# Block attention put between the blocks of two gate projections

## The chip, the cores and the metric

One core of one Trainium2 chip. The metric is the device time of one execution in microseconds (us): the median of three runs.

## What is computed

Two transformer-like blocks run one behind the other on 256 tokens of width 2048, all in float32. The first is latent attention and an mLSTM layer. The change lies in the second block:

```
mod  = silu(c) @ w_ada + b_ada                    # six rows of 2048, "ada"
h    = rms_norm(x, norm1) * (1 + sc1) + sh1
qa, ka, va, qb, kb, vb, ga, gb = split(h @ w_in)
ya   = softmax(qa ka' * scale) va                 # 8 heads on 2 key heads, all 256 keys
yb   = softmax(qb kb' * scale + bias) vb          # 8 heads, neighbourhood of 16 columns
merged = sigmoid(ga) * (ya @ w_oa) + sigmoid(gb) * (yb @ w_ob)
x    = x + g1 * (merged @ w_out)
```

A feed-forward layer of width 5632 and a last norm follow. Each head has 128 columns. A unit of the attention is one head and one of the two blocks of 128 queries, so there are 32 units.

## The kernel before

The weights of all projections come through one ring of four slots. A block is 128 rows by 1024 columns of a weight, 512 KB. SP (SyncE) loads it into `raw` when the slot was rounded the last time (`lo_ready`). ACT rounds it to `hi` (`hi_block`, line 545; it waits for the landing and until PE is done with the block four before). DVE writes what rounding left, `raw - hi`, to `lo` (`lo_block`, line 919). PE multiplies in three passes, hi x XH, lo x XH and hi x XL, where XH and XL are the two parts of the activations: 12 matmuls of 512 columns for a block (`token_major`, line 1644), which then counts `block_done`. Blocks are numbered through the kernel; `B_MERGE` is the first of the gates.

PSUM has eight banks of 512 columns. They are used as two halves, group 0 and group 1, of four banks. A projection accumulates in one half over 16 blocks, while the other half is evicted. `TURN_PLAN` (line 78) gives each projection its half (`@0` or `@1` sets it, else they alternate) and who evicts it. `start` (line 1634) makes PE wait until the last user of its half was evicted.

Beside the projections runs the ada product: 384 pieces of 128x512, 256 KB each, which POOL loads into a second ring of four slots (`ada_raw`) and DVE adds up, one instruction for a piece (`ada_block`, line 924). `ADA_BESIDE` (line 129) says how many pieces stand beside which projection; `rest_blocks` (line 954) spreads them over the blocks 4 to 15 of it, each behind the block's rounding. Pieces are taken in one fixed order, so a changed number moves all that follow.

All engines run lists written out by hand, with semaphores between them. Around the change the order is: the projections qa, kva, qb, kb, vb; the row g1; the transposes qaT and kaT; the attention (lines 1722 for PE, 629 for ACT, 1039 for DVE), which runs alone, with three of the four ring slots rounded, and uses all eight banks; then the four gate projections ga0, ga1, gb0 and gb1, with 16 blocks each; oa0, ob0, oa1 and ob1 with 8 each; the transposes of `merged`; and wo0 and wo1 with 16 each.

The attention is a pipeline over units. PE computes the scores (L1732), DVE adds the bias for units of b (L1505) and takes the maximum (L1048), ACT takes the exponential (L646), PE turns it (L1742), ACT copies it (L639), PE multiplies it with the values (L1753), DVE divides by the sum (L1053, L1063), PE turns the pair of a head back (L1762), and ACT and DVE write its two parts (L651, L1073).

The mLSTM stage has a similar pattern already: in mz0 and mz1 PE computes a head's scores (L1843, L1849, L1850) and values (L1864) behind every fourth block.

Of the kernel before, what the change touches and what calls it, by code (L numbers as in the profile page):

```python
# [13 lines left out]
P = 128  # L14
# [34 lines left out]
for _name, _n in (("ident", 128), ("inv_freq", 32), ("causal", 256), ("window", 64), ("toeplitz", 191),  # L49
# [36 lines left out]
    "biasa:act biasb:act ada1:dve hTa@1:split4 hTb:split4 qa:act kva:act qb:act kb:act vb:act g1:act qaT:act kaT:act "  # L86
    "ga0@0:act ga1:act gb0:act gb1:act oa0:dve ob0:dve oa1:dve ob1:dve mTa:split4 wo0:dve mTb:split4 wo1@0:dve "

# [35 lines left out]
for _name in GROUP:  # L124
    if _name not in LAST_BLOCK and _name not in BANKS_BEFORE:
# [4 lines left out]
              "mo_1": 20, "mz0": 6, "mz1": 6, "lo0": 16,  # L130
              "qa": 16, "kb": 8, "vb": 16, "ga0": 22, "ga1": 22, "gb0": 22, "gb1": 22, "oa0": 6, "ob0": 6, "oa1": 6,
              "ob1": 6, "wo0": 20, "wo1": 20}
ADA_FIRST = {}
for _name, _n in ADA_BESIDE.items():
    ADA_FIRST[_name] = sum(ADA_BESIDE[_m] for _m in ADA_FIRST)
N_UNITS = sum(ADA_BESIDE.values()) // KD


def two_block_kernel(nc, positions, x, xT, pack, const, gate_b, qk_norm, rpbT, mla_w_in, mla_w_qb, mla_w_kvb,
# [4 lines left out]
    with ExitStack() as ctx:  # L144
# [61 lines left out]
        vb_tok = at("vb_tok", 168, [P, TOK, N_A * HD])  # L206
        sig_a = at("sig_a", 168, [P, TOK, D])
        sig_b = at("sig_b", 184, [P, TOK, D])
        kva_tok = at("kva_tok", 176, [P, TOK, 4, HD])
# [3 lines left out]
        probT2 = at("probT2", 197, [P, 2, SEQ])  # L213
        y_tok2 = at("y_tok2", 199, [P, 4, P])
        merged = sig_a
# [88 lines left out]

        A1, A3 = att_sems("mla"), att_sems("blk")

        def bank(S, n):

            return ((n + 4) % 8 if S is A1 else n) * HALF
        M2 = {n: sem(f"ml_{n}") for n in ("prep", "prepc", "st", "bc", "arg", "exp", "w", "pv", "h", "sq", "y",  # L310
# [225 lines left out]
        def _(act):  # L536
# [92 lines left out]
            def attention(S, units, pr, prT, nm, rs, keys, H):  # L629

                for i in range(units + 6):
                    if 2 <= i < units + 2:
                        u = i - 2
                        nk = keys(u)
                        b = bank(S, 3 + u % 2)
                        act.wait_ge(S["turned"], u + 1)
                        if u >= 2:
                            act.wait_ge(S["summed"], u - 1)
                        nc.scalar.copy(prT[:, u % 2, 0:nk], ps[:, b:b + nk]).then_inc(S["copied"], 1)  # L639
                    if i < units:  # L640
                        u = i
                        nk = keys(u)
                        act.wait_ge(S["maxed"], u + 1)
                        if u >= 3:
                            act.wait_ge(S["turned"], u - 2)
                        nc.scalar.activation(pr[:, u % 3, 0:nk], ps[:, bank(S, u % 3):bank(S, u % 3) + nk], ACT.Exp,  # L646
                                             bias=nm[:, u:u + 1], accum_out=rs[:, u:u + 1]).then_inc(S["exped"], 1)
                    if i >= 6 and i % 2 == 0:
                        h = (i - 6) // 2
                        act.wait_ge(S["backed"], h + 1)  # L650
                        nc.scalar.copy(H(h), ps[:, bank(S, 7):bank(S, 7) + SEQ]).then_inc(S["hi"], 1)  # L651

# [156 lines left out]
            for tok in range(TOK):  # L809
# [27 lines left out]
            rest(B_MERGE, 16)  # L837
            for n, (name, sig) in enumerate((("ga0", sig_a), ("ga1", sig_a), ("gb0", sig_b), ("gb1", sig_b))):
                first4(B_MERGE + 16 * (n + 1))
                c0 = n % 2 * COLS  # L840
                each_tok(name, lambda t: sig[:, t, c0:c0 + COLS], ACT.Sigmoid)
                rest(B_MERGE + 16 * (n + 1), 16 if n < 3 else 8)
            for n in range(3):
# [60 lines left out]
        def _(dve):  # L904
# [48 lines left out]

            def rest_blocks(n0, b0, b1, nb, name=None, hooks=(), before=lambda b: None, beside=None):

# [83 lines left out]
            def attention(S, units, nm, rs, ri, yt, keys, prepare, gate, H, L):  # L1039
                inverse = {}  # L1040
                for i in range(units + 6):
                    if i < units:
                        u = i
                        nk = keys(u)
                        b = bank(S, u % 3)
                        dve.wait_ge(S["scored"], u + 1)
# [8 lines left out]
                    if 4 <= i < units + 4:  # L1055
                        u = i - 4
                        b = bank(S, 5 + u % 2)
                        after(inverse[u])
# [11 lines left out]
                    if i >= 7 and i % 2 == 1:  # L1070
                        h = (i - 7) // 2
                        dve.wait_ge(S["hi"], h + 1)
                        nc.vector.tensor_tensor(L(h), ps[:, bank(S, 7):bank(S, 7) + SEQ], H(h).bitcast(F32),  # L1073
                                                ALU.subtract) \
# [432 lines left out]

            attention(A3, 32, nmax2, rsum2, rinv2, y_tok2, lambda u: SEQ, add_bias, None,
                      lambda h: yaH[:, h, :] if h < N_A else ybH[:, h - N_A, :],
                      lambda h: yaL[:, h, :] if h < N_A else ybL[:, h - N_A, :])  # L1510
            lo_block(B_MERGE + 3, 3)
            rest(B_MERGE, 16, "ga0")
            for n, name in enumerate(("ga1", "gb0", "gb1")):
                first4(B_MERGE + 16 * (n + 1))
                rest(B_MERGE + 16 * (n + 1), 16, name)
            first4(B_MERGE + 64)
            rest(B_MERGE + 64, 8, "oa0")
            def merge_columns(name, q, first_tok):

                for tok in range(TOK):  # L1520
                    if tok == 0:
                        after(first_tok)
                    else:
                        dve.wait_ge(freed_sem["dve"], FREED[name][1])
                    m = merged[:, tok, q * COLS:(q + 1) * COLS]
                    nc.vector.tensor_tensor(m, m, sig_b[:, tok, q * COLS:(q + 1) * COLS], ALU.add) \
                      .then_inc(ev("merged"), 1)

            for n, name in enumerate(("oa0", "ob0", "oa1", "ob1")):
# [6 lines left out]
                for tok in range(TOK):  # L1536
                    v = sig[:, tok, q * COLS:(q + 1) * COLS]
                    ins = nc.vector.tensor_tensor(v, v, T(name, tok), ALU.mult)
# [92 lines left out]
        def _(pe):  # L1631
# [90 lines left out]
            def attention(S, units, pr, prT, yt, keys, operands, values):  # L1722
                for i in range(units + 6):
                    if i < units:
                        u = i
                        nk = keys(u)
                        b = bank(S, u % 3)
                        if u >= 3:
# [6 lines left out]
                    if 2 <= i < units + 2:  # L1735
                        u = i - 2
                        b = bank(S, 3 + u % 2)
                        pe.wait_ge(S["exped"], u + 1)
# [6 lines left out]
                    if 3 <= i < units + 3:  # L1745
                        u = i - 3
                        b = bank(S, 5 + u % 2)
                        pe.wait_ge(S["copied"], u + 1)
# [7 lines left out]
                    if i >= 6 and i % 2 == 0:  # L1756
# [4 lines left out]
                        for tok in range(TOK):  # L1761
                            ins = nc.tensor.transpose(ps[:, bank(S, 7) + tok * P:bank(S, 7) + (tok + 1) * P],  # L1762
                                                      yt[:, (2 * h + tok) % 4, :], ident[:, :])
# [159 lines left out]

            def blk_operands(u):
                h, blk = (u % 16) // 2, u % 2
                t = slice(blk * P, (blk + 1) * P)
                if u < 16:
                    return [(qaT[:, h, t], kaT[:, h // (N_A // N_KV), :])]
                return [(qbT[:, h, t], kbT[:, h, :])]

            def blk_values(u, t):
                h = (u % 16) // 2
                return kva_tok[:, t, N_KV + h // (N_A // N_KV), :] if u < 16 else vb_tok[:, t, h * HD:(h + 1) * HD]

            attention(A3, 32, prob2, probT2, y_tok2, lambda u: SEQ, blk_operands, blk_values)
            pe.wait_ge(A3["lo"], 16)
            for n, name in enumerate(("ga0", "ga1", "gb0", "gb1")):
                token_major(name, B_MERGE + 16 * n, 16, XH, XL)
# [3 lines left out]
            transposes("mTa", operand_tiles(merged, 0))  # L1942
# [3 lines left out]
            transposes("mTb", operand_tiles(merged, 8))  # L1946
            token_major("wo0", B_WO, 16, XH, XL, m_tiles, blocks=(5, 16))
# [104 lines left out]
```

## Time and profile before

| | |
|---|---|
| runs | 2322.74, 2323.46, 2320.55 us; median 2322.74 |
| profiled execution | 2328.05 us, its span 2326.0 us |
| mean granted TensorE clock | 0.978 |
| PE busy | 2242.2 us, 96% of the span |
| DVE busy | 1495.8 us, 64% |
| ACT busy | 1010.2 us, 43% |
| moved by the queues | 499.25 MB, mean 215 GB/s |

The span runs from the first to the last instruction of the program; the run's time has a few us around it. Busy shares are means over stages with different limits; the stages around the change are in the rows below. PE's busy time is modelled and overlaps from one matmul to the next, so the start times of the matmuls say more than the durations. In a row of busy time by stretch stand its start and end, its length, the busy time of PE, of PE's weight loads, DVE, ACT and POOL with the number of instructions, then the granted clock as a share of full speed, the busy share of the queues and their GB/s. In a row of a group stand its busy time and the mean ns of one instruction, then the idle time of the engine before them. In a timeline, x2 is two instructions put together, and one float32 matmul of the attention is two instructions.

### The profile page before, as it was taken

To read this page: it belongs to the slowest core of one execution; us is meant where nothing else is said; L and a number is where in the kernel's file an instruction comes from. 1 tells how busy PE (TensorE), PEld (TensorE's weight loads), DVE (VectorE), ACT (ScalarE), POOL (GpSimd) and SP (SyncE) were. 2 spreads that over 40 slices of the span, in tenths; PEclk is the share of its full clock that TensorE was granted. 3 is DMA by queue.
4 is the path that set the end of the run, shared out by engine and by line. 5 is a ranking of instruction groups with operands and counts; after the bars stand their busy time and mean duration, and the time that the engine had idled before them with its cause. 6 is when DMAs were issued, how large, how long until landed. Compare 5 with 4: busy or idle time off the path is not lost.

```text
span 2326.0 us, 33356 instructions
## 1 busy us (share of the span) xinstructions
PE 2242.2 (96%) x11044; PEld 1886.3 (81%) x11044; DVE 1495.8 (64%) x1990; ACT 1010.2 (43%) x1248; POOL 243.3 (10%) x425
## 2 busy tenths in 40 slices
PE   8999997999999979999999999989999999999997
PEld 6888776997877768899777878878888888888885
DVE  5666577897776866678677778875454444444544
ACT  5444534444444434443544433444344444443432
POOL 1110011212220030101112221110000000000000
PEclk9999999999999997999999999999999999999998
DMA  8786067787986583767449888764656656666563
GB/s 304 249 239 179 28 226 253 243 267 265 315 272 180 157 246 118 257 182 235 162 140 313 305 305 276 260 228 145 190 189 191 190 184 196 190 193 206 188 198 120
DMA packets 196667, 499.25 MB, mean 215 GB/s; under 512 B 29785, under 2 KB 56537, under 8 KB 195649
## 3 DMA queue, kind: packets, MB, share of 16 engines
q1 hardware_dynamic: 163648, 388.03, 51.6%
q0 software_dynamic: 32896, 109.55, 14.4%
q8 instruction: 82, 1.34, 0.2%
q14 instruction: 41, 0.33, 0.0%
HBM read 495.34 MB, written 2.10 MB: 214 GB/s over the span
## 4 chain that ended last, share of the span: by engine, by line
PE 74%; DMA 10%; DVE 8%; issue 4%; ACT 3%; POOL 1%; POOLq 0%; DVEq 0%; SPq 0%; ACTq 0%
PE ps L1663 59%; PE ps L1672 7%; DMA ada_raw<-in_w_ada_dram 7%; DVE lo L921 3%; PE ps L1732 2%; DVE acc_s L933 2%; DMA raw<-in_ml_w_in_dram 1%; PE ps L1753 1%; PE ps L1823 1%; ACT hi L549 1%; DVE acc_g L933 1%; PE ps L1742 1%; DMA raw<-in_w_in_dram 1%; DVE conv_tmp L1225 1%; DMA rel<-in_rpbT_dram 1%
## 5 line engine op out<-in xcount | busy, mean ns | idle before, releaser
L921 DVE TENSOR_TENSOR lo<-raw,hi 128x1024 fp32r<-128x1024 f32 x732 | 890.5, 1223 | 576.6 <-ACT hi L549 574.5
L549 ACT CAST hi<-raw 128x1024 fp32r<-128x1024 f32 x732 | 768.0, 1054 | 1089.3 <-PE ps L1663 770.2
L1663 PE MATMUL ps<-hi,XH 128*128 128x512 f32 x2080 | 652.3, 394 | 38.9 <-DVE lo L921 31.3
L1663 PE MATMUL ps<-lo,XH 128*128 128x512 f32 x2080 | 646.3, 391 | 0.0
L1663 PE MATMUL ps<-hi,XL 128*128 128x512 f32 x2080 | 645.4, 390 | 0.0
L1663 PEld LDWEIGHTS ps<-hi,XH 128*128 128x128 f32 x2080 | 388.5, 189 | 125.9 <-DVE lo L921 27.2
L1663 PEld LDWEIGHTS ps<-hi,XL 128*128 128x128 f32 x2080 | 392.1, 189 | 82.8
L1663 PEld LDWEIGHTS ps<-lo,XH 128*128 128x128 f32 x2080 | 392.1, 189 | 82.6
L463 POOL DMA_DIRECT2D ada_raw<-in_w_ada_dram x384 | 206.9, 539 | 1190.6 <-DVE acc_s L933 811.1
L933 DVE SCALAR_TENSOR_TENSOR acc_s<-ada_raw,c_act,acc_s 128x512 f32<-128x512 f32 x256 | 191.5, 748 | 47.2 <-DMA ada_raw<-in_w_ada_dram 45.0
L1672 PE MATMUL ps<-XH,hi 128*128 (+1 forms) x512 | 145.0, 283 | 1.1 <-DVE XL L1037 1.1
L1672 PE MATMUL ps<-XH,lo 128*128 (+1 forms) x512 | 144.9, 283 | 0.0
L1672 PE MATMUL ps<-XL,hi 128*128 (+1 forms) x512 | 144.9, 283 | 0.0
L933 DVE SCALAR_TENSOR_TENSOR acc_g<-ada_raw,c_act,acc_g 128x512 f32<-128x512 f32 x128 | 95.8, 749 | 37.4 <-DMA ada_raw<-in_w_ada_dram 36.6
L1663 PE MATMUL ps<-hi,FH 128*128 128x512 f32 x352 | 108.5, 389 | 0.0
L1663 PE MATMUL ps<-lo,FH 128*128 128x512 f32 x352 | 108.4, 389 | 0.0
L1663 PE MATMUL ps<-hi,FL 128*128 128x512 f32 x352 | 108.3, 389 | 0.0
L1672 PEld LDWEIGHTS ps<-XH,hi 128*128 128x128 f32 x512 | 98.3, 192 | 1.4 <-DVE XL L1037 1.4
L1672 PEld LDWEIGHTS ps<-XL,hi 128*128 128x128 f32 x512 | 98.3, 192 | 0.0
L1672 PEld LDWEIGHTS ps<-XH,lo 128*128 128x128 f32 x512 | 98.3, 192 | 0.0
L1663 PEld LDWEIGHTS ps<-lo,FH 128*128 128x128 f32 x352 | 66.1, 188 | 13.8
L1663 PEld LDWEIGHTS ps<-hi,FL 128*128 128x128 f32 x352 | 66.1, 188 | 13.7
(311 smaller groups left out, 1676.8 us busy)
## 6 DMA issues: line engine op xcount, KB each, us to landing
ada_raw<-in_w_ada_dram POOLq DMA_DIRECT2D x384, 256.0 KB, 5.1
raw<-in_w_in_dram SPq DMA_DIRECT2D x136, 512.0 KB, 4.6
raw<-in_ml_w_in_dram SPq DMA_DIRECT2D x128, 512.0 KB, 5.0
raw<-in_w_gate_dram SPq DMA_DIRECT2D x176, 256.0 KB, 2.8
raw<-in_w_up_dram SPq DMA_DIRECT2D x176, 256.0 KB, 3.0
raw<-in_w_down_dram SPq DMA_DIRECT2D x88, 512.0 KB, 3.7
raw<-in_mla_w_in_dram SPq DMA_DIRECT2D x48, 512.0 KB, 5.3
raw<-in_mla_w_out_dram SPq DMA_DIRECT2D x32, 512.0 KB, 4.7
```

What stands on the lines that cost most here:

```text
L463: pool.dma_start(ada_raw[:, j, :], w_ada[0][bass.ds((RING * g + j) * P, P), bass.ds(u * HALF, HALF)]) \
L549: nc.scalar.copy(hi[:, j, :], raw[:, j, :]).then_inc(hi_ready, 1)
L921: nc.vector.tensor_tensor(lo[:, j, :], raw[:, j, :], hi[:, j, :].bitcast(F32), ALU.subtract) \
L933: nc.vector.scalar_tensor_tensor(out=acc, in0=ada_raw[:, m % RING, :], scalar=c_act[:, k:k + 1], in1=acc, op0=ALU.mult, op1=ALU.add).then_ ...
L1225: ins = nc.vector.scalar_tensor_tensor(out=conv_tmp[:, k, s:], in0=ps[:, g + k * SEQ:g + (k + 1) * SEQ - s], scalar=col("conv_w", (TAPS - ...
L1663: ins = mm(ps[:, o:o + HALF], x, w[:, j, c0:c0 + HALF], start=first, stop=(k == nb * per_block - 1 and x is xl), skip_group_check=True)
L1672: ins = mm(ps[:, o:o + SEQ], w[:, j, m * P:(m + 1) * P], x(k), start=first and lead and m % 2 == 0, stop=last and w is lo, skip_group_chec ...
L1732: ins = mm(ps[:, b:b + nk], q, kk, start=(n == 0), stop=(n == len(ops) - 1), skip_group_check=True)
L1742: ins = nc.tensor.transpose(ps[:, b + t * P:b + (t + 1) * P], pr[:, u % 3, t * P:(t + 1) * P], ident[:, :])
L1753: ins = mm(ps[:, b:b + P], prT[:, u % 2, t * P:(t + 1) * P], values(u, t), start=(t == 0), stop=(t == n - 1), skip_group_check=True)
L1823: ins = mm(ps[:, o:o + 1], acc_s[:, vec, k * P:(k + 1) * P], ones[:, 0:1], start=True, stop=True, skip_group_check=True)
```

## The change

Attention and gates are merged into one stage. The attention is cut into 36 steps, which stand behind the first 31 gate blocks: one behind each, and two behind the blocks 3, 6, 9, 12 and 15. The units of b come first, then those of a.

In a step i, PE computes the scores of unit i, the values of head (i-4)/2 if i is even, and turns unit i-2. ACT rounds block b+4, then takes the exponential of unit i and, in odd steps, copies both turned units of a head in one instruction; in even steps it writes the high part of a head's result. DVE adds the bias and takes the maximum of unit i ahead of the rounding of block b+4, and behind this rounding and its ada pieces it divides unit i by its sum and, in odd steps, writes the low part of a result.

The division is now on the probabilities, 256 columns in SBUF, ahead of their transposes. The value matmuls have the values as weights and 256 queries as columns, so that the result comes out turned; the transposes back are gone. The attention needs four banks (4 to 7): two for scores, one for the turned probabilities, one for the result. The gates ga0, ga1 and gb0 all accumulate in group 0. The sigmoids of ga0 and ga1 are evicted ahead of the rounding of the blocks 19 and 35.

Ada pieces: ga0 has 12 instead of 22; qa has 18 instead of 16, kva 4 instead of none, and wo0 and wo1 have 22 each instead of 20. `sig_a`, `sig_b` and `merged` are laid out by column half first. The rest of the diff is the function `bank`, which has lost an argument.

```diff
-    "ga0@0:act ga1:act gb0:act gb1:act oa0:dve ..."
+    "ga0@0:act ga1@0:act gb0@0:act gb1:act oa0:dve ..."
-              "qa": 16, "kb": 8, "vb": 16, "ga0": 22, "ga1": 22, "gb0": 22, "gb1": 22, ... "wo0": 20, "wo1": 20}
+              "qa": 18, "kva": 4, "kb": 8, "vb": 16, "ga0": 12, "ga1": 22, "gb0": 22, "gb1": 22, ... "wo0": 22, "wo1": 22}
+STEPS_AFTER = {}
+_step = 0
+for _block in range(31):
+    _n = 2 if _block in (3, 6, 9, 12, 15) else 1
+    STEPS_AFTER[_block] = tuple(range(_step, _step + _n))
+    _step += _n
...
+        def score_slot(u):
+            return (4 + u % 2) * HALF
+        turn_slot, value_slot = 6 * HALF, 7 * HALF
...
@@ ACT
-            attention(A3, 32, prob2, probT2, nmax2, rsum2, lambda u: SEQ,
-                      lambda h: yaH[:, h, :] if h < N_A else ybH[:, h - N_A, :])
+            def blk_step(i):
+                if i < 32:
+                    act.wait_ge(A3["maxed"], i + 1)
+                    if i >= 3:
+                        act.wait_ge(A3["turned"], i - 2)
+                    o = score_slot(i)
+                    nc.scalar.activation(prob2[:, i % 3, :], ps[:, o:o + SEQ], ACT.Exp, bias=nmax2[:, i:i + 1],
+                                         accum_out=rsum2[:, i:i + 1]).then_inc(A3["exped"], 1)
+                if i >= 3 and i % 2 and i < 34:
+                    h = (i - 3) // 2
+                    act.wait_ge(A3["turned"], 2 * h + 2)
+                    if h:
+                        act.wait_ge(A3["summed"], h)
+                    nc.scalar.copy(probT2[:, :, :].rearrange(flat), ps[:, turn_slot:turn_slot + HALF]) \
+                      .then_inc(A3["copied"], 1)
+                if i >= 4 and i % 2 == 0:
+                    h = (i - 4) // 2
+                    H, _, hh = blk_head(h)
+                    act.wait_ge(A3["summed"], h + 1)
+                    nc.scalar.copy(H[:, hh, :], ps[:, value_slot:value_slot + SEQ]).then_inc(A3["hi"], 1)
...
+            for b in range(4, 48):
+                if b == 19:
+                    act.wait_ge(A3["summed"], N_A)
+                    gate("ga0", sig_a, 0)
+                if b == 35:
+                    act.wait_ge(A3["summed"], 2 * N_A)
+                    gate("ga1", sig_a, 1)
+                hi_block(B_MERGE + b, b % RING, landed(B_MERGE + b, b % RING))
+                for i in STEPS_AFTER.get(b - 4, ()):
+                    blk_step(i)
@@ DVE, rest_blocks
                     done = b - start - RING
                     for m in range(count * done // (nb - RING), count * (done + 1) // (nb - RING)):
                         ada_block((ADA_FIRST[name] + m) // KD, (ADA_FIRST[name] + m) % KD)
+                    behind(b)
@@ DVE
+            def blk_maximum(i):
+                if i < 32:
+                    o = score_slot(i)
+                    dve.wait_ge(A3["scored"], i + 1)
+                    add_bias(i, o)
+                    nc.vector.tensor_reduce(nmax2[:, i:i + 1], ps[:, o:o + SEQ], AX_X, ALU.max, negate=True) \
+                      .then_inc(A3["maxed"], 1)
+            def blk_divide(i):
+                if i < 32:
+                    dve.wait_ge(A3["exped"], i + 1)
+                    link(nc.vector.reciprocal(rinv2[:, i:i + 1], rsum2[:, i:i + 1]))
+                    nc.vector.tensor_scalar(prob2[:, i % 3, :], prob2[:, i % 3, :], rinv2[:, i:i + 1], None,
+                                            ALU.mult).then_inc(A3["normed"], 1)
+                if i >= 5 and i % 2:
+                    h = (i - 5) // 2
+                    H, L, hh = blk_head(h)
+                    dve.wait_ge(A3["hi"], h + 1)
+                    nc.vector.tensor_tensor(L[:, hh, :], ps[:, value_slot:value_slot + SEQ],
+                                            H[:, hh, :].bitcast(F32), ALU.subtract).then_inc(A3["lo"], 1)
...
@@ PE
+            def blk_step(i):
+                if i < 32:
+                    ...
+                    if i >= 2:
+                        pe.wait_ge(A3["exped"], i - 1)
+                    o = score_slot(i)
+                    mm(ps[:, o:o + SEQ], q, k, start=True, stop=True, skip_group_check=True).then_inc(A3["scored"], 1)
+                if i >= 4 and i % 2 == 0:
+                    h = (i - 4) // 2
+                    pe.wait_ge(A3["copied"], h + 1)
+                    if h >= 1:
+                        pe.wait_ge(A3["lo"], h)
+                    ...
+                        ins = mm(ps[:, o:o + SEQ], v, probT2[:, t, :], start=(t == 0), stop=(t == TOK - 1),
+                                 skip_group_check=True)
+                    ins.then_inc(A3["summed"], 1)
+                if 2 <= i < 34:
+                    u = i - 2
+                    pe.wait_ge(A3["normed"], u + 1)
+                    if u >= 2 and u % 2 == 0:
+                        pe.wait_ge(A3["copied"], u // 2)
+                    for t in range(TOK):
+                        o = turn_slot + t * SEQ + u % 2 * P
+                        ins = nc.tensor.transpose(ps[:, o:o + P], prob2[:, u % 3, t * P:(t + 1) * P], ident[:, :])
+                    ins.then_inc(A3["turned"], 1)
...
+            for n, name in enumerate(("ga0", "ga1", "gb0")):
+                token_major(name, B_MERGE + 16 * n, 16, XH, XL, then=blk_after(16 * n))
             pe.wait_ge(A3["lo"], 16)
```

## Rows read from the trace of the kernel before

**Rows 1.** Busy time by stretch: attention, two gates, two gates, wo.
```profile
1142.76:1187.32 44.56, 41.61 (x281) 34.92 (x280) 36.89 (x125) 31.26 (x109) 0.00 (x0) 0.99 0.01 2
1187.32:1279.35 92.03, 89.92 (x384) 72.92 (x385) 66.17 (x75) 36.39 (x35) 26.04 (x46) 0.98 0.83 286
1279.35:1371.25 91.90, 88.23 (x384) 71.72 (x385) 68.09 (x77) 37.17 (x36) 23.67 (x44) 1.00 0.89 306
...
1461.69:1558.00 96.31, 92.46 (x406) 74.55 (x407) 76.17 (x86) 37.57 (x40) 19.37 (x36) 1.00 0.77 260
```

**Rows 2.** Timeline of PE: start, duration; two units of attention, a gate block.
```profile
1144.31 0.60 PE L1732 MATMUL ps<-kaT,qaT 128*128 128x256 f32 x2
1144.74 0.38 PE L1742 MATMUL ps<-ident,prob 128*128 128x128 f32 x2
1144.96 0.61 PE L1753 MATMUL ps<-kva_tok,probT 128*128 128x128 f32 x4
...
1193.17 0.62 PE L1663 MATMUL ps<-hi,XH 128*128 128x512 f32 x2
...
1195.90 0.61 PE L1663 MATMUL ps<-hi,XH 128*128 128x512 f32 x2
```

**Rows 3.** Waits of PE in the gates: us in total, times, longest.
```profile
PE ps L1663 <- DVE lo L921: 5.6, 6, 1.6
```

**Rows 4.** Timeline of PE in mz0: one head between four blocks.
```profile
696.84 0.69 PE L1843 MATMUL ps<-ge,select 8*128 8x256 f32 x2
697.46 0.70 PE L1849 MATMUL ps<-qkT 128*128 128x256 f32 x2
698.00 0.38 PE L1850 MATMUL ps<-qkT 128*128 128x128 f32 x2
...
706.43 1.46 PE L1864 MATMUL ps<-mv,decay 128*128 128x257 f32 x6
...
710.54 0.69 PE L1843 MATMUL ps<-ge,select 8*128 8x256 f32 x2
```

**Rows 5.** Groups by line in the attention: count, busy us, mean ns.
```profile
L646 ACT ACTIVATE prob<-ps,nmax 128x256 f32<-128x256 f32 x30 | 14.3, 478 | 7.1 <-DVE nmax L1048 7.1
L1048 DVE TENSOR_REDUCE nmax<-ps 128x1 f32<-128x256 f32 x30 | 12.7, 425 | 6.0 <-PE ps L1732 5.3
...
L1505 DVE TENSOR_TENSOR ps<-ps,na_bias 128x256 f32<-128x256 f32 x16 | 9.5, 591 | 0.0
...
L646 ACT ACTIVATION_READ_ACCUMULATOR prob<-ps,nmax 128x1 f32 x30 | 5.9, 198 | 0.0
L1053 DVE RECIPROCAL rinv<-rsum 128x1 f32<-128x1 f32 x31 | 4.8, 153 | 0.0
...
L1073 DVE TENSOR_TENSOR ybL<-ps,ybH 128x256 fp32r<-128x256 f32 x8 | 3.4, 419 | 1.4 <-ACT ybH L651 1.4
```

**Rows 6.** Groups by line in the four gates: rounding and ada pieces.
```profile
L921 DVE TENSOR_TENSOR lo<-raw,hi 128x1024 fp32r<-128x1024 f32 x62 | 75.1, 1220 | 14.4 <-ACT hi L549 14.3
L549 ACT CAST hi<-raw 128x1024 fp32r<-128x1024 f32 x64 | 67.5, 1055 | 110.3 <-DMA raw<-in_w_in_dram 58.2 <-PE ps L1663 45.6 <-DMA raw<-in_w_oa_dram 6.5
L933 DVE SCALAR_TENSOR_TENSOR acc_s<-ada_raw,c_act,acc_s 128x512 f32<-128x512 f32 x88 | 65.9, 749 | 35.3 <-DMA ada_raw<-in_w_ada_dram 34.4
```

**Rows 7.** Timeline of ACT at the eviction of ga0.
```profile
1235.19 1.28 ACT L586 ACT_TABLE_LOAD   x1
1236.49 1.94 ACT L586 ACTIVATE sig_a<-ps 128x1024 f32<-128x1024 f32 x2
```

**Rows 8.** Groups by line elsewhere: a scaling in SBUF, a copy from PSUM.
```profile
L1408 DVE TENSOR_SCALAR h_norm<-X,ry 128x2048 f32<-128x2048 f32 x2 | 2.6, 1286 | 0.1
...
L806 ACT COPY na_bias<-ps 128x480 f32<-128x480 f32 x6 | 3.0, 569 | 8.0 <-PE ps L1906 8.0
```

**Rows 9.** Busy time by stretch, behind the tail and behind a wait.
```profile
1187.90:1191.80 3.90, 3.90 (x12) 3.03 (x11) 1.12 (x1) 0.00 (x0) 0.00 (x0) 0.56 0.39 105
...
1361.80:1365.80 4.00, 3.99 (x18) 3.28 (x19) 3.81 (x5) 1.13 (x2) 1.16 (x3) 1.00 0.83 273
```

More of the change, by code:

```diff
@@ L86 @@
     "biasa:act biasb:act ada1:dve hTa@1:split4 hTb:split4 qa:act kva:act qb:act kb:act vb:act g1:act qaT:act kaT:act "
-    "ga0@0:act ga1:act gb0:act gb1:act oa0:dve ob0:dve oa1:dve ob1:dve mTa:split4 wo0:dve mTb:split4 wo1@0:dve "
+    "ga0@0:act ga1@0:act gb0@0:act gb1:act oa0:dve ob0:dve oa1:dve ob1:dve mTa:split4 wo0:dve mTb:split4 wo1@0:dve "
     "g2:act ada2:dve h2Ta:split4 h2Tb:split4").split() \
@@ L130 @@
               "mo_1": 20, "mz0": 6, "mz1": 6, "lo0": 16,
-              "qa": 16, "kb": 8, "vb": 16, "ga0": 22, "ga1": 22, "gb0": 22, "gb1": 22, "oa0": 6, "ob0": 6, "oa1": 6,
-              "ob1": 6, "wo0": 20, "wo1": 20}
[2 rows of a table added]
 ADA_FIRST = {}
@@ L206, in two_block_kernel @@
         vb_tok = at("vb_tok", 168, [P, TOK, N_A * HD])
-        sig_a = at("sig_a", 168, [P, TOK, D])
-        sig_b = at("sig_b", 184, [P, TOK, D])
+        sig_a = at("sig_a", 168, [P, 2, TOK, COLS])
+        sig_b = at("sig_b", 184, [P, 2, TOK, COLS])
         kva_tok = at("kva_tok", 176, [P, TOK, 4, HD])
@@ L650, in attention @@
                         act.wait_ge(S["backed"], h + 1)
-                        nc.scalar.copy(H(h), ps[:, bank(S, 7):bank(S, 7) + SEQ]).then_inc(S["hi"], 1)
+                        nc.scalar.copy(H(h), ps[:, bank(7):bank(7) + SEQ]).then_inc(S["hi"], 1)
             for q in range(4):
@@ L833, in _ @@
             whole("kaT", kaT[:, :, :].rearrange(flat), width=2 * SEQ)
-            attention(A3, 32, prob2, probT2, nmax2, rsum2, lambda u: SEQ,
-                      lambda h: yaH[:, h, :] if h < N_A else ybH[:, h - N_A, :])
-            fourth(B_MERGE)
[L837 to L842, printed above, removed]
+            def blk_step(i):
[18 more added lines that the diff above has]
+                    nc.scalar.copy(H[:, hh, :], ps[:, value_slot:value_slot + SEQ]).then_inc(A3["hi"], 1)
@@ new lines, in gate @@
+            def gate(name, sig, q):
+                each_tok(name, lambda t: sig[:, q, t, :], ACT.Sigmoid)
+            fourth(B_MERGE)
+            for b in range(4, 48):
[8 more added lines that the diff above has]
+                    blk_step(i)
@@ L843, in _ @@
+            for n, (name, q) in enumerate((("gb0", 0), ("gb1", 1))):
+                first4(B_MERGE + 16 * (n + 3))
+                gate(name, sig_b, q)
+                rest(B_MERGE + 16 * (n + 3), 16 if n < 1 else 8)
             for n in range(3):
@@ L952, in rest, with rest_blocks @@
                 rest_blocks(n0, RING, nb, nb, name, hooks)
-            def rest_blocks(n0, b0, b1, nb, name=None, hooks=(), before=lambda b: None, beside=None):
+            def rest_blocks(n0, b0, b1, nb, name=None, hooks=(), before=lambda b: None, beside=None,
+                            behind=lambda b: None):
                 name, start = beside or (name, 0)
@@ L1044, in attention @@
                         nk = keys(u)
-                        b = bank(S, u % 3)
+                        b = bank(u % 3)
                         dve.wait_ge(S["scored"], u + 1)
@@ L1056, in attention @@
                         u = i - 4
-                        b = bank(S, 5 + u % 2)
+                        b = bank(5 + u % 2)
                         after(inverse[u])
@@ L1511, in _, with blk_before, do, blk_behind @@
+            def blk_before(off):
+                def do(b):
+                    for i in STEPS_AFTER.get(off + b - 4, ()):
+                        blk_maximum(i)
+                return do
+            def blk_behind(off):
+                def do(b):
+                    for i in STEPS_AFTER.get(off + b - 4, ()):
+                        blk_divide(i)
+                return do
             lo_block(B_MERGE + 3, 3)
-            rest(B_MERGE, 16, "ga0")
+            rest_blocks(B_MERGE, 4, 16, 16, "ga0", before=blk_before(0), behind=blk_behind(0))
@@ L1513, in _ @@
             for n, name in enumerate(("ga1", "gb0", "gb1")):
-                first4(B_MERGE + 16 * (n + 1))
-                rest(B_MERGE + 16 * (n + 1), 16, name)
+                n0, before, behind = B_MERGE + 16 * (n + 1), blk_before(16 * (n + 1)), blk_behind(16 * (n + 1))
+                for b in range(RING):
+                    before(b)
+                    lo_block(n0 + b, b)
+                    behind(b)
+                rest_blocks(n0, 4, 16, 16, name, before=before, behind=behind)
@@ L1524, in merge_columns @@
                         dve.wait_ge(freed_sem["dve"], FREED[name][1])
-                    m = merged[:, tok, q * COLS:(q + 1) * COLS]
-                    nc.vector.tensor_tensor(m, m, sig_b[:, tok, q * COLS:(q + 1) * COLS], ALU.add) \
+                    m = merged[:, q, tok, :]
+                    nc.vector.tensor_tensor(m, m, sig_b[:, q, tok, :], ALU.add) \
                       .then_inc(ev("merged"), 1)
@@ L1726, in attention @@
                         nk = keys(u)
-                        b = bank(S, u % 3)
+                        b = bank(u % 3)
                         if u >= 3:
@@ L1736, in attention @@
                         u = i - 2
-                        b = bank(S, 3 + u % 2)
+                        b = bank(3 + u % 2)
                         pe.wait_ge(S["exped"], u + 1)
@@ L1746, in attention @@
                         u = i - 3
[L1747 removed]
+                        b = bank(5 + u % 2)
                         pe.wait_ge(S["copied"], u + 1)
@@ L1936, in _, with blk_after, do @@
+            def blk_after(off):
+                def do(b):
+                    for i in STEPS_AFTER.get(off + b, ()):
+                        blk_step(i)
+                return do
+            for n, name in enumerate(("ga0", "ga1", "gb0")):
+                token_major(name, B_MERGE + 16 * n, 16, XH, XL, then=blk_after(16 * n))
             pe.wait_ge(A3["lo"], 16)
-            for n, name in enumerate(("ga0", "ga1", "gb0", "gb1")):
-                token_major(name, B_MERGE + 16 * n, 16, XH, XL)
+            token_major("gb1", B_MERGE + 48, 16, XH, XL)
@@ L1941, in _ @@
             pe.wait_ge(ev("merged"), 2)
-            transposes("mTa", operand_tiles(merged, 0))
+            transposes("mTa", operand_tiles(merged[:, 0], 0))
             m_tiles = lambda k: (tile_split, SPLIT_BASE["mTa"] + k // 2 + 1)
@@ L1945, in _ @@
             pe.wait_ge(ev("merged"), 4)
-            transposes("mTb", operand_tiles(merged, 8))
+            transposes("mTb", operand_tiles(merged[:, 1], 0))
             token_major("wo0", B_WO, 16, XH, XL, m_tiles, blocks=(5, 16))
```

47 lines of the change are left out of this document (22 added, 25 removed), and 2 rows, old and new, of the table ADA_BESIDE.

## Prediction, made before the changed kernel was run

> **What bounds the kernel now.** I read the stage sums first, then the TensorE timeline inside them, then the groups of the two other engines. PE is the bound. Two matmuls of 512 columns start 0.453 us after the two before, and a block of 12 lasts 2.73 us, 1193.17 to 1195.90 [rows 2]; call it 2.72. The 64 gate blocks need 174.1 us and take 92.03 + 91.90 = 183.9 [rows 1]: 4.99 too many in the first two gates, 4.86 in the last two. The first 1.9 are half clock after the attention's tail: 12 matmuls from 1187.90 to 1191.80, at 0.56 [rows 9]. Most of the rest are six waits of PE for a rounded block, 5.6 us [rows 3], with the queues at 286 and 306 GB/s. The attention takes 44.56 us in front, with 2 GB/s on the queues, since the ring is full and nobody frees a slot. So the hope in this place is not only PE's waits inside the attention but also the empty queues.
>
> **What leaves.** The stretch 1142.76 to 1187.32, 44.56 us, and the 4.99 us of the first two gates: their blocks will be further apart, and 34 ada pieces with 32 blocks at some 5 us each ask for (17 + 9) MB / 160 us, about 160 GB/s, half of what the queues gave [rows 1]. Sum -49.55.
>
> **What PE gets between the blocks.** A score matmul takes 0.43 us of PE, 1144.31 to 1144.74; two transposes 0.22, to 1144.96 [rows 2]. Now there are 32 scores (13.8), 32 pairs of transposes (7.0), and 16 value steps of two 256-column matmuls, each priced like a score (0.86 each, 13.8). The transposes of the result go. That is 34.6 us. Entering and leaving is extra. The mlstm stage has the same pattern: 13.70 us from one L1843 to the next for four blocks (10.88) and two insertions [rows 4], so 2.82 for matmuls of 256 + 256 + 128 + 3 x 257 columns, which at 0.43 per 256 are 2.37. So 0.23 per insertion, and 30 of the 31 blocks have one: 6.9. Sum +41.5. Already here the gain is nearly gone: 49.55 against 41.5. PE was busy in 41.61 of the old 44.56 us [rows 1], and its own work can't be hidden beside PE.
>
> **What PE waits for.** Step i stands behind block b on PE, but on DVE its maximum stands ahead of the rounding of block b+4, and its division and the low part (L) behind that rounding and the ada pieces. The value matmuls of head h, in step 2h+4, overwrite the value bank and so wait for L of head h-1, which DVE does at the end of step 2h+3; and for ACT's copy of step 2h+3. Behind the waiting value matmul stand the step's transposes and all further blocks. In five blocks (3, 6, 9, 12, 15) both steps come together, the odd one first, so the whole DVE group lies between two neighbouring PE instructions.
>
> Blocks 6 and 9, from the end of the block: the score is readable at 0.7 (0.1 entry, 0.60 duration). DVE then needs two bias additions and two maxima (2 x (0.591 + 0.425) = 2.03), a rounding (1.22), one ada piece (0.75) [rows 5, 6], reciprocal 0.15, the division of 128x256 and L 0.42. The division in SBUF is in no row. Below it lies the reciprocal of one column (0.15), above the bias addition on PSUM (0.59). I take 0.31: the reciprocal's fixed 0.15 and 0.63 ns a column from 1286 ns for 2048 [rows 8]. DVE is done at 5.6; PE is there at 0.1 + 0.43 + 0.22 + 0.43 = 1.2. Wait 4.4, twice 8.8. Block 12: one bias addition, no ada piece: 4.2, wait 3.0. Block 3: no L yet, but the copy of both tiles on ACT: 0.7 + 1.02, exponential 0.48 + 0.20, copy 0.57 (480 columns [rows 8]) = 3.0, wait 1.8. Block 15: ACT first evicts ga0, loading the sigmoid's table (1.28 + 1.94 [rows 7]), rounds a block (1.05), loads the exponential's table again (1.28), exponential 0.68: 6.2; then DVE 0.88: 7.1, wait 5.9. Together 19.5.
>
> Single blocks: from a value step at T the next odd score is readable at T + 0.86 + 0.22 + 0.12 + 2.72 + 0.1 + 0.60 = T + 4.6, DVE's odd group takes 3.87 with bias and one ada piece, 4.02 without bias and two; PE is back at T + 8.04. Waits of 0.45 three times, 0.6 four times: 3.8. Even groups end in time.
>
> ga0, ga1 and gb0 now share one half of PSUM. Before ga1 the eviction is in the 5.9 above. Before gb0 nothing covers it: table 1.28, two activations 1.94, restart 0.2: 3.4.
>
> All of these waits: 26.7. Bounds: 10, if most of what I count as serial overlaps (the rows give durations, not spacings); 32 with the division at 0.59 and semaphores of 0.1 each.
>
> Here the Trainium skill speaks against the change harder than the trace. ScalarE: Activation LUTs, "What ACT_TABLE_LOAD costs", adds a drain of about 1.38 us to each switch of tables. The rows don't show it: the load starts at 1235.19, lasts 1.28, and the first sigmoid starts at 1236.49 [rows 7]. By the page, three exposed switches would add 4.1 us.
>
> **The clock.** After a wait of under 2 us it stays full: 1.00 in 1361.80:1365.80. Behind the attention's tail, in which PE pauses between short matmuls, it fell for 4 us, and cost 1.9 [rows 9]. Five of my waits are 3 us or longer. Bounds 0 and 5 x 1.9 = 9.5; I take 3, as they are between the two rows.
>
> **The ada pieces.** Ten leave ga0. Six go to qa and kva, where PE has no wait; 18 pieces beside 12 blocks are fewer than the 22 that the gates carry at a loss of 2.5 a gate: 0. Four go to wo0/wo1, which have 96.31 us for 87.0 of blocks and 1.9 of transposes: 7.4 lost to a rounding chain that waits for transfers. Each piece is 0.262 MB; four at 286 GB/s are 3.7 us, at most; 0 if prefetched. I take 3, since the stage already loses. POOL issues them in the same order, and its wait for g1 comes before ga0 as before. SP's loads wait for each rounding, which comes later than now, but three rounded blocks (8 us and more) stand ahead of PE. The merged layout of sig_a and sig_b costs nothing: same counts, same sizes. Losses in gb0 and gb1: 4.86 as before, since the ring holds four blocks and can't save up.
>
> **Sum.** -49.55 + 41.5 + 19.5 + 3.8 + 3.4 + 3 + 3 = +24.7 us. The profiled execution took 2328.05 with a span of 2326.0; the changed span would be 2350.7. It ran 5.3 above the median of 2322.74, and I put the difference on the median: 2347.4.
>
> **Rivals.** (a) The forecast, 2347, its own range 2334 to 2360: 0.66. (b) The clock falls after every long wait: 9.5 in place of 3, and the slower blocks make the next DVE group relatively early, so no more: 2354. For it the 0.56 behind the tail, against it the 1.00 behind 1.6 us of waiting. 0.14. The Trainium skill, TensorE: Matmul & The Clock Gate, "HAM oscillation", says the same of a kernel with a wait in each pass: the half clock is paid again after each. By it (b) is the rule and not the exception; whether 4 us are enough, no row here shows. (c) DVE is well ahead: it finishes the rounding while the score runs, and half of the 23.3 of chain waits vanish, with the clock whole and wo unmoved: 2347.4 - 11.6 - 6 = 2330. 0.08. (d) The other side: the value matmuls never wait. The place is the doubled step, the price 23.3, and it decides where DVE's group ends within 1.2 us of the block. For it: the mlstm pattern repeats at 13.70 without a wait [rows 4]. Against: there each head's pieces lie three blocks apart, here the group is 3 to 5 us. Then -49.55 + 41.5 + 3.4 + 3 = -1.7, and with rested queues gb0 loses nothing, -2.4: 2322.7 - 4.1 = 2318.6; with the entries cheaper by half, 2315. Say 2317. 0.12. That the change doesn't do what it says I rule out: the queue orders are in the code.
>
> **Numbers.** 0.2% is 4.6 us, about what a measurement of this kernel can tell from no change. (a), (b) and (c) are slower, 0.88, less 0.03 for their lower edges; (d) splits into 0.02 same and 0.10 faster. So faster 0.10, same 0.05, slower 0.85. The range leaves out most of (d) and the far side of (b): 2328 to 2362.
>
> **What would show it.** In the changed trace PE waits in front of the value matmuls, for DVE's low parts, some 4 us at blocks 6 and 9 and near 6 at block 15; about 3.3 us idle before gb0; three ACT table loads where there was one behind the attention; queues well under 286 GB/s in ga0 and ga1; more waits in wo1. It is wrong if the stretch from the first score to the first oa0 matmul (228.5 us now) is under 240 us, if PE's waits sum to under 10 us there, or if entries cost other than 0.23.

## The result, and the profile after

The changed kernel takes 2353.82 us (median of 4 runs, 2352.6 to 2358.88), the kernel before 2321.64 beside it. The ratio is 1.0145, 95% interval 1.0130 to 1.0159: slower by 1.45%. The profiled execution's span is 2350.9 us, against 2326.0.

Where the 24.9 us of span are, by start times on PE. hTa and h2Ta are the transposes of `h` ahead of qa and ahead of the feed-forward layer.

| stretch | before | after |
|---|---|---|
| start to the transposes hTa | 922.8 | 920.0 |
| hTa to the first oa0 matmul (the change) | 448.4 | 471.3 |
| first oa0 matmul to the transposes h2Ta (oa, ob, wo) | 202.2 | 207.4 |
| the rest | 752.5 | 752.3 |

Busy time by stretch of the changed kernel: attention with ga0 and ga1; gb0 and gb1; wo; the few single-column matmuls behind wo. They answer to [rows 1].

```profile
1137.09:1296.40 159.31, 134.51 (x576) 106.37 (x576) 102.44 (x194) 68.66 (x133) 19.25 (x35) 0.94 0.53 162
1296.40:1391.26 94.86, 89.84 (x386) 72.92 (x385) 66.41 (x76) 37.96 (x37) 23.59 (x44) 0.98 0.81 280
1481.69:1582.06 100.37, 94.80 (x408) 74.57 (x408) 80.11 (x90) 37.49 (x40) 21.46 (x40) 1.00 0.77 262
1582.06:1598.67 16.61, 13.68 (x65) 13.68 (x65) 7.44 (x18) 6.06 (x6) 0.00 (x0) 0.57 0.20 64
```

The first row is the point: 159 us in which PE is idle for 24.8 us, at a mean clock of 0.94, with the queues at 162 GB/s. No engine and no queue is full. The waits of PE in this stage (us in total, times, longest), where [rows 3] had only the rounded blocks:

```profile
PE ps L2033 <- DVE ybL L1581: 18.7, 7, 6.1
PE ps L2033 <- DVE yaL L1581: 4.6, 6, 1.4
PE ps L1754 <- ACT sig_a L605: 3.4, 1, 3.4
PE ps L1754 <- DVE lo L972: 1.6, 3, 0.9
PE ps L2033 <- ACT probT L868: 1.6, 1, 1.6
```

L2033 are the value matmuls, L1581 is the low part of the head before. One doubled block in order of time, block 6 (start us, duration):

```profile
1166.46 0.59 PE L2023 MATMUL ps<-kbT,qbT 128*128 128x256 f32 x2
1166.72 1.05 ACT L568 CAST hi<-raw 128x1024 fp32r<-128x1024 f32 x1 [2.49 <-PE ps L1754]
...
1167.09 0.61 DVE L1558 TENSOR_TENSOR ps<-ps,na_bias 128x256 f32<-128x256 f32 x1 [1.47 <-PE ps L2023]
1167.11 0.60 PE L2023 MATMUL ps<-kbT,qbT 128*128 128x256 f32 x2
...
1168.66 0.58 ACT L868 COPY probT<-ps 128x512 f32<-128x512 f32 x1
1168.69 0.42 DVE L1567 TENSOR_REDUCE nmax<-ps 128x1 f32<-128x256 f32 x1
1169.03 1.22 DVE L972 TENSOR_TENSOR lo<-raw,hi 128x1024 fp32r<-128x1024 f32 x1
...
1170.16 0.74 DVE L984 SCALAR_TENSOR_TENSOR acc_s<-ada_raw,c_act,acc_s 128x512 f32<-128x512 f32 x1
...
1171.02 0.35 DVE L1575 TENSOR_SCALAR prob<-prob,rinv 128x256 f32<-128x256 f32 x1
1171.29 0.42 DVE L1581 TENSOR_TENSOR ybL<-ps,ybH 128x256 fp32r<-128x256 f32 x1
...
1171.85 2.04 PE L2033 MATMUL ps<-probT,vb_tok 128*128 128x256 f32 x4 [4.14 <-DVE ybL L1581]
```

Both scores are there at 1167.7, ACT's copy ends at 1169.2, but the value matmul starts at 1171.85, 0.14 us after the end of L. Between them DVE has done all that the order puts ahead of L: two biases, two maxima, a rounding, an ada piece, a division.

### The profile page after: what moved, and what is told of

It is laid out like the page before. It is cut to its first block, busy times and chain, and to the rows that moved or that the text cites. A ratio compares the mean times of both kernels' runs of the same rounds, so it can differ in the third digit from the quotient of the medians.

```text
span 2350.9 us, 33027 instructions
## 1 busy us (share of the span) xinstructions
PE 2242.6 (95%) x10948; PEld 1882.3 (80%) x10948; DVE 1499.8 (64%) x1990; ACT 1007.7 (43%) x1234; POOL 243.3 (10%) x425
## 3 DMA queue, kind: packets, MB, share of 16 engines
q0 software_dynamic: 32896, 109.55, 14.2%
## 4 chain that ended last, share of the span: by engine, by line
PE 74%; DVE 10%; DMA 8%; issue 4%; ACT 3%; POOL 1%; POOLq 0%; DVEq 0%; ACTq 0%; SPq 0%
PE ps L1754 60%; PE ps L1763 7%; DMA ada_raw<-in_w_ada_dram 5%; DVE lo L972 3%; DVE acc_s L984 2%; DMA raw<-in_ml_w_in_dram 2%; PE ps L1914 1%; ACT hi L568 1%; PE ps L1823 1%; DVE acc_g L984 1%; PE ps L2033 1%; DVE conv_tmp L1278 1%; DMA rel<-in_rpbT_dram 1%; PE ps L1844 0%; PE ps L1792 0%
## 5 line engine op out<-in xcount | busy, mean ns | idle before, releaser
L482 POOL DMA_DIRECT2D ada_raw<-in_w_ada_dram x384 | 207.1, 539 | 1200.9 <-DVE acc_s L984 825.9
```

Of the source, the lines that this page charges most:

```text
L482: pool.dma_start(ada_raw[:, j, :], w_ada[0][bass.ds((RING * g + j) * P, P), bass.ds(u * HALF, HALF)]) \
```

## The experiments

The edits are to the changed kernel unless it says otherwise. The second and fourth columns below come from start times in each run's trace: the stretch from hTa to the first oa0 matmul, and the one from there to h2Ta.

| run | hTa to oa0 | PE's waits for L, copy or division | oa0 to h2Ta | time, ratio to before |
|---|---|---|---|---|
| before | 448.4 | - | 202.2 | |
| changed | 471.3 | 24.8 | 207.4 | 2353.8, 1.0145 |
| l_first | 451.4 | 11.9 | 205.4 | 2330.7, 1.0051 [1.0032, 1.0069] |
| even_odd | 454.1 | 8.8 | 207.9 | 2332.6, 1.0049 [1.0033, 1.0065] |
| both | 439.1 | 0 | 207.4 | 2317.3, 0.9986 [0.9971, 1.0000] |
| before_new_ada | 445.8 | - | 207.1 | 2326.6, 1.0008 [0.9989, 1.0027] |
| no_sigmoid | 472.5 | 22.8 | 206.4 | 2348.7, 1.0125 [1.0106, 1.0144] |
| both_old_ada | 451.5 | 6.9 | 202.0 | 2320.9, 0.9998 [0.9982, 1.0015] |
| both_half | 434.0 | 0 | 205.7 | 2311.3, 0.9959 [0.9945, 0.9973] |
| both_half_old_ada | 446.6 | 7.6 | 201.5 | 2315.7, 0.9978 [0.9966, 0.9990] |

Medians of different sessions are compared by the ratios only. The start of the program up to hTa, which is no part of the stretches, took 915.9 to 922.8 us in these ten traces, though no edit touches what runs there; differences of some us ahead of hTa are not the edits'.

**l_first.** The low part is moved to the head of its step on DVE.

```diff
             def blk_maximum(i):
+                if i >= 5 and i % 2:
+                    ... (the five lines that write L)
                 if i < 32:
...
             def blk_divide(i):
...
-                if i >= 5 and i % 2:
-                    ...
```

> The changed kernel with one edit: in an odd step DVE writes the low part of a result (L) first, ahead of the maximum, instead of last, behind the rounding, the ada pieces and the division. Theory A (the value matmul waits for DVE's whole group because L stands at its end): what is left to wait for is ACT's copy, 1.6 to 2.1 us in the blocks 6, 9 and 12 (4.1, 4.1 and 2.9 in the changed kernel), about 5.7 at block 15 (6.1), and under 0.3 in the single blocks, which had 5.5 together. Waits 24.8 to about 13, and a little less half clock: 2341 us, against 2354. Rival B (the copy, behind rounding and exponential on ACT, ends nearly as late as L): the waits keep over 21 us, and the time is 2350 or more.

PE's waits:

```profile
PE ps L2033 <- ACT probT L868: 11.9, 5, 5.6
PE ps L1754 <- ACT sig_a L605: 3.4, 1, 3.4
PE ps L1754 <- DVE lo L972: 1.7, 1, 1.7
```

The waits are for ACT's copy now, 1.6 in four doubled blocks and 5.6 at block 15, and none is left in the single blocks. B falls. Theory A stands, and was too modest: 451.4 is 19.9 less, and the waits are only 12.9 of it. About 4 of the other 7 are the clock. The changed kernel lost 4.7 us to half clock at the blocks 6, 9 and 12, and 1.6 in the first gate block, where this run lost nothing; but behind the 5.6 and behind the 3.4 ahead of gb0 this run lost 2.8 and 2.7 us, against 1.6 and 1.7. The 1.6 of the first gate block are chance, since nothing that stands ahead of that block was edited. Another 2 are later starts: a value step that waits takes 0.24 us more than its wait, and nine single steps no longer wait. From the score at 1161.48 in the changed kernel to the next block at 1163.61 are 2.13 us, with a wait of 0.46; a step without one takes 1.43.

The first gate block in the changed kernel and here, both behind the same wait of 1.65, and the stretch behind the 5.6:

```profile
1137.09:1140.00 2.91, 2.91 (x7) 2.27 (x8) 1.23 (x1) 0.84 (x1) 0.26 (x1) 0.54 0.60 182
...
1135.06:1138.00 2.94, 2.94 (x13) 2.43 (x14) 1.23 (x1) 0.84 (x1) 0.26 (x1) 1.00 0.62 180
...
1212.36:1218.30 5.94, 5.94 (x15) 4.70 (x16) 1.00 (x4) 0.79 (x3) 0.00 (x0) 0.50 0.31 88
```

**even_odd.**

```diff
-    _n = 2 if _block in (3, 6, 9, 12, 15) else 1
+    _n = 2 if _block in (2, 5, 8, 11, 14) else 1
```

> The changed kernel with one edit: the five double steps stand behind the blocks 2, 5, 8, 11 and 14 instead of 3, 6, 9, 12 and 15, so that the even step comes first and the step whose copy and low part the value matmul needs is always one block back. Theory A (the waits of the doubled blocks are a chain between two neighbouring PE instructions): the five waits of 18.8 us together fall to under 2 us each, since a block of 2.7 us now lies between; the eviction of ga0, which the two steps behind block 15 had covered, shows with about 2 us ahead of ga1; less half clock. 2337 us. Rival C (DVE has no time to spare in this stage, and the waits only show where it is late): the waits move to other steps and keep over 20 us in sum, 2350 us.

```profile
PE ps L1754 <- ACT sig_a L605: 5.2, 2, 3.4
PE ps L2033 <- DVE yaL L1581: 4.6, 6, 1.4
PE ps L2033 <- DVE ybL L1581: 4.2, 6, 0.9
```

The long waits of the doubled blocks are gone. Twelve value steps wait 0.2 to 1.4 us, three of them, with 0.5 each, in the doubled blocks 5, 8 and 11; and the eviction of ga0 shows with 1.85 us. C falls: the same instructions in another order, and 14.2 us fewer waits for DVE and ACT's copy, net of the eviction.

**both.** The two edits together.

> Both edits: L first, and the even step first in the doubled blocks. Theory A: value matmuls wait for under 3 us in all; about 2 us ahead of ga1 and 3.4 ahead of gb0 stay, and the half clock of about 6 us goes with the waits. 2353.8 - 22 - 6 + 1 = 2327 us, a little above the kernel before. Rival C (DVE out of time): 2345 us or more. If it comes out under the kernel before, the entries of PE between blocks cost less than I took (0.23 us each).

Value matmuls don't wait at all. What is left are the evictions of ga0 and ga1:

```profile
PE ps L1754 <- ACT sig_a L605: 5.2, 2, 3.4
PE ps L1754 <- DVE lo L972: 1.8, 1, 1.8
```

439.1 is 32.2 under the changed kernel and 9.3 under the one before; 5 of these are lost again behind oa0. The time is level with before, 10 us better than I expected. The stretch gained 32.2 where my sum had 27. The waits gave 22.9 net of ga0's eviction and the clock 6.4, about as forecast; what the sum lacked are the later starts, 14 times 0.24 us. The other 5 of the 10 don't lie in this stretch, and the profiled execution, the slowest of ten, doesn't show them.

**before_new_ada.** The kernel before, with the new ada counts.

```diff
-"qa": 16, ... "ga0": 22, ... "wo0": 20, "wo1": 20
+"qa": 18, "kva": 4, ... "ga0": 12, ... "wo0": 22, "wo1": 22
```

> The kernel before with the ada counts of the changed one alone (ga0 12 instead of 22; qa +2, kva +4, wo0 +2, wo1 +2). Theory A (wo is late through its transfers): nothing in qa and kva, ga0 loses up to 2 us less, wo0 and wo1 lose 3 to 5 us more: 2321.6 + 2 = 2324 us. Rival D (wo's loss in the changed kernel, 5.2 us, comes from the state in which the gates leave the rings, not from the four pieces): wo as before, and the time at or up to 2 us under the kernel before.

The stretch to h2Ta is 4.9 longer, nearly as in the changed kernel (5.2); 4.5 of it lie inside wo, up to the matmuls of the row g2. That part takes 94.1 us in the kernel before, 92.6 and 94.3 in the other two traces with 20 pieces beside each projection, and 96.8 to 99.5 in all seven with 22. So the loss in wo is that of the four pieces, and D falls. The stretch to oa0 gains 2.6: 1.5 in the gates, and 1.1 at the start of the attention, where the clock stayed full here and fell in the kernel before. As a whole the shift costs about nothing: its interval includes 1.

**no_sigmoid.** It leaves out the sigmoids of ga0 and ga1.

```diff
-                each_tok(name, lambda t: sig[:, q, t, :], ACT.Sigmoid)
+                each_tok(name, lambda t: sig[:, q, t, :], ACT.Sigmoid if sig is sig_b else None)
```

> The changed kernel with ga0 and ga1 evicted as plain copies: it leaves out the two sigmoids of ga, and with them three loads of the function table (sigmoid, exponential again, sigmoid) on ACT; nothing else moves. Theory A (the table loads lie in full in the two waits): the wait at block 15 falls from 6.1 to 3.5 us (two loads of 1.28), the one ahead of gb0 from 3.4 to 2.1, and gb0's eviction loads the table itself, under cover. 2354 - 4 = 2350 us, less if the clock recovers sooner. By the Trainium skill (ScalarE: Activation LUTs, What ACT_TABLE_LOAD costs) each switch also has a drain of 1.38 us, and the waits would fall by 5.3 and 2.7 us. Rival E (ACT is late through the rounding and the exponential, the loads are hidden behind DVE's group): the wait at block 15 stays over 5 us.

The wait at block 15 falls from 6.10 to 4.08, the one ahead of gb0 from 3.37 to 2.07. So the load ahead of gb0 shows in full (1.30 for 1.28). Of the two at block 15, 2.0 of 2.56 us show: in the changed kernel DVE's reciprocal waited 0.65 us for the exponential behind the second load, and here it follows DVE's rounding without a wait. E falls. The stretch isn't shorter all the same: the clock was low for longer behind three of the waits. The span is 3.9 us shorter, and 4.1 us of difference lie ahead of hTa, where nothing was edited; so the better time (two runs only) is not shown to be the sigmoids'.

```profile
PE ps L2033 <- DVE ybL L1581: 16.6, 7, 4.1
...
PE ps L1754 <- ACT sig_a L609: 2.1, 1, 2.1
```

The drain that the Trainium skill adds to a switch (ScalarE: Activation LUTs, "What ACT_TABLE_LOAD costs") shows nowhere: load at 1296.48 for 1.28, activation at 1297.78, in the changed kernel's trace of ACT:

```profile
1296.48 1.28 ACT L605 ACT_TABLE_LOAD   x1 [1.66 <-PE ps L1754]
1297.78 1.94 ACT L605 ACTIVATE sig_a<-ps 128x1024 f32<-128x1024 f32 x2
```

**both_old_ada.** Both, with the ada counts of before.

> L first and the even step first, as in the run called both, and besides the ada counts of the kernel before (22 pieces beside ga0 again; 16 beside qa, none beside kva, 20 beside wo0 and wo1). Theory A (DVE's group no longer lies between PE instructions, so pieces beside ga0 cost nothing, and wo gets back its 5 us): value matmuls wait for under 2 us in all, wo loses 5 us less: 2317 - 4.5 = 2312.5 us. Rival C (DVE is then full: a group with two pieces and a bias takes 4.6 us and more against a step of about 4.0 on PE): waits of 5 us or more come back in ga0, and the time is 2317 or more.

wo has its 5 us back (202.0), but ga0 takes 78.0 us instead of 67.9, and 2320.9 is what C expected. Waits for divisions and copies, 6.9 us, come back in ga0. One of them, 2.5 us, isn't DVE's load at all (see the last section).

**both_half.** Both, and gb0 in the half that the attention has left.

```diff
-    "ga0@0:act ga1@0:act gb0@0:act gb1:act ... mTb:split4 wo1@0:dve "
+    "ga0@0:act ga1@0:act gb0@1:act gb1:act ... mTb:split4 wo1@1:dve "
...
-            for n, name in enumerate(("ga0", "ga1", "gb0")):
+            for n, name in enumerate(("ga0", "ga1")):
                 token_major(name, B_MERGE + 16 * n, 16, XH, XL, then=blk_after(16 * n))
             pe.wait_ge(A3["lo"], 16)
+            token_major("gb0", B_MERGE + 32, 16, XH, XL)
```

> The run called both, and besides gb0 accumulates in the half of PSUM that the attention has just left, so that it need not wait for ga1's eviction; PE waits for the last low part ahead of gb0 instead of ahead of gb1, and every later projection uses the other half than before. Theory A (the 3.4 us and the half clock behind them are the price of three gates in one half): the wait falls to under 0.5 us and the half clock in gb0 goes, 2317.3 - 3.4 - 1.5 = 2312.5 us. Rival F (gb0 and gb1 are bound by their transfers anyway, and the wait only let the queues get ahead): the wait goes and comes back as waits for rounded blocks in gb0 and gb1, 2316 us or more.

```profile
PE ps L1754 <- DVE lo L972: 3.2, 3, 1.5
PE ps L1754 <- ACT sig_a L605: 1.9, 1, 1.9
```

The wait of 3.4 is gone and with it the half clock behind it (3.0 us in both); 1.4 us come back as waits for rounded blocks (3.2 against 1.8), and the clock of the stage is 1.00. 434.0 is 5.1 less. F is right only in those 1.4. This version beats both kernels: 0.41% under the one before, interval 0.27% to 0.55%.

```profile
1137.07:1296.00 158.93, 156.34 (x720) 128.50 (x721) 125.16 (x220) 84.24 (x150) 27.59 (x51) 1.00 0.69 219
```

In the same 159 us as the changed kernel's first row above PE does 720 matmul instructions instead of 576.

**both_half_old_ada.**

> All of it: L first, even step first, gb0 in the other half, ada counts of the kernel before. Theory A: the two gains add up, 2308 us, 0.6% under the kernel before. Rival F or C: 2313 us or more.

The gains of the half remain, those of the ada counts don't: 7.6 us of waits in ga0. C again.

## Why the prediction was right

It forecast 2347 and slower; 2353.8 came, inside the range, and the span was forecast as 2350.7 and is 2350.9. The mechanism is shown by l_first, even_odd and both. But the exact hit of the span is luck of terms that cancel, and one of the prediction's own signs of being wrong has come: entries cost other than 0.23.

| term | forecast | measured |
|---|---|---|
| the attention leaves | -44.6 | -47.4 |
| losses of ga0 and ga1 leave | -5.0 | -5.0 |
| attention's work on PE | 41.5 | 36.0 |
| waits in doubled blocks | 19.5 | 18.8 |
| waits in single blocks | 3.8 | 5.9 |
| later starts, 14 x 0.24 | 0 | 3.4 |
| ahead of gb0 | 3.4 | 3.4 |
| half clock behind the waits | 3 | 7.8 |
| half clock in the first gate block | 0 | 1.6 |
| losses in gb0 and gb1 | 0 | -2.1 |
| wo and behind | 3 | 5.2 |
| sum | +24.7 | +27.6 |

The work on PE came 5.5 lower and the clock 6.4 higher than forecast. Of the rest, 0.5 lies in the stretch unplaced, and -2.8 ahead of hTa, where executions differ by more than that.

*What leaves.* The prediction starts the attention at 1142.76. The first score is at 1139.91, so three scores and a pair of transposes, 2.85 us at a clock of 0.56, leave too; and its "228.5 us now" from the first score to oa0 is 231.3 (249.8 in the changed kernel). In gb0 and gb1, 91.5 us from 1299.77 less 87.0 of blocks and 1.7 of half clock leave 2.8 of losses, where the kernel before had 4.86: PE waits 1.6 us for rounded blocks in the four gates now, not 5.6 [rows 3].

*The work between the blocks.* An odd step without a wait costs 0.70 (a block at 1258.08, the next at 1261.50, less 2.72), an even one 1.55 (1215.12 to 1219.39): 16 x 2.25 = 36.0. I took 0.88 and 1.74. An entry costs under 0.1 here, not the 0.23 of [rows 4]. The mlstm's matmuls have other shapes, and I charged their difference to the entry; that this is all of it no run shows.

*Doubled blocks.* Waits 1.60, 4.14, 4.14, 2.85 and 6.10 against 1.8, 4.4, 4.4, 3.0 and 5.9. The division took 0.35, I had 0.31; each chain of DVE overlaps a little.

*Single blocks.* Three of 0.47 in ga0 (0.45 forecast), then 0.16 or 0.95, by whether one or two ada pieces stand in the odd group, and 1.38 at the last. I had 0 and 0.6. PE comes back sooner than I reckoned: 5.44 + 2.25 = 7.69 from one value step to the next, not 8.04, for the same cheaper entries.

*The clock* is, with the attention's work, the term that was most mis-sized. Its 7.8 + 1.6 are nearly the 9.5 of rival (b), whose 2354 is also the time that came. Granted clock behind the wait at block 6, at block 12, and around the last single one of 1.38 us:

```profile
1171.85:1175.00 3.15, 3.15 (x9) 2.54 (x10) 0.41 (x1) 0.37 (x1) 0.32 (x1) 0.52 0.67 228
...
1209.00:1212.00 3.00, 3.00 (x8) 2.44 (x9) 0.31 (x1) 0.37 (x1) 0.00 (x0) 0.50 0.60 175
...
1277.90:1282.90 5.00, 3.62 (x18) 2.70 (x16) 4.03 (x8) 3.03 (x5) 1.07 (x3) 1.00 0.69 234
```

It fell to 1.2 GHz behind all five waits of 2.85 us or more, each of which cost another 1.5 to 1.7 us. The other traces say the same of this stage: 14 of 14 such waits, with up to 2.8 us lost behind one. Behind value steps that waited 1.6 or less it stayed full in every trace. Between these it went either way: behind the 1.65 ahead of the first gate block it fell in three traces of eight, behind the 1.85 ahead of ga1 in one of five, behind the 2.07 ahead of gb0 in no_sigmoid it fell, and behind the 2.50 of both_old_ada but not of both_half_old_ada. In these two, in this order:

```profile
1157.65:1161.06 3.41, 3.41 (x10) 2.66 (x9) 3.34 (x6) 0.83 (x3) 0.69 (x2) 0.50 0.42 95
...
1154.53:1158.00 3.47, 3.47 (x17) 2.87 (x18) 3.37 (x7) 1.02 (x4) 1.07 (x2) 1.00 0.34 109
```

What the Trainium skill tells (TensorE: Matmul & The Clock Gate, "HAM oscillation"), that a wait in each pass buys the half clock each time, held here for the long waits, and I weighed it too low.

*wo.* 2.7 in the stretch, near my 3. Another 2.5 lies behind it, where I had not looked: 0.8 in PE's wait for the eviction of wo (2.94 against 2.17), and 1.7 in the 64 single-column matmuls, 13.8 us instead of 12.1, at a clock of 0.57 instead of 0.65. The 1.7 are not the pieces': the same matmuls take 12.2 in before_new_ada, and 10.9 to 13.8 in the traces with the same counts. Why the clock differs there no run shows.

*Rivals.* (d) said the value matmuls never wait; they did, 14 times. The run both takes the waits away and measured 2317.3, the 2317 that I gave to (d), partly by chance: ga0's eviction showed and gb0 was not relieved, but entries were cheaper.

## What to carry to other kernels

When work is threaded between the matmuls of another stage, write down for each of its waits what the releasing engine has in its queue ahead of the release, and move the release to the front of it: here one instruction of 0.42 us, moved past a rounding and a division, was worth some 20 us. A step that depends on its neighbour must not share a gap with it. Keep PE's waits short even if their sum stays: behind each of 3 us or more came another 1.5 to 2.8 of loss at half clock.

## What the runs showed of the hardware that was not expected

In both_old_ada and in both_half_old_ada one division of 128x256 in SBUF took 2.33 us instead of 0.35, while POOL's memset of 128x2048 ran, and ended 0.15 us after it. The other 31 divisions took 0.35 to 0.46, and a rounding (two sources) beside a longer memset of POOL's (128x4096) took its usual 1.22 in the changed kernel. DVE and POOL, both_old_ada:

```profile
1154.62 2.33 DVE L1581 TENSOR_SCALAR prob<-prob,rinv 128x256 f32<-128x256 f32 x1
1154.98 1.82 POOL L495 MEMSET acc_g<- 128x2048 f32 x1
...
1157.01 0.44 PE L2043 MATMUL ps<-ident,prob 128*128 128x128 f32 x2 [2.50 <-DVE prob L1581]
```

With the new counts the memset runs at 1132.9, ahead of the gates, where DVE has nothing to do. The same is seen in every trace beside the memset of 128x4096 that POOL does near hTa: there a cast of 128x512 from SBUF to SBUF took 1.6 to 1.75 us instead of 0.42 and ended just behind the memset. The kernel before:

```profile
923.03 3.51 POOL L476 MEMSET acc_s<- 128x4096 f32 x1 [73.50 <-PE ps L1823]
...
925.08 1.75 DVE L1036 CAST XH<-tmp 128x512 fp32r<-128x512 f32 x1 [0.68 <-ACT tmp L610]
927.47 0.42 DVE L1036 CAST XH<-tmp 128x512 fp32r<-128x512 f32 x1
```

So instructions with one source in SBUF were held, and the rounding with two sources was not; why, no run here separates.
